# Eight of twelve `w_ada` column blocks summed on GpSimd instead of multiplied on TensorE, in a transformer block on one Trainium2 core

## What is computed

```python
cond = jax.nn.silu(c)                                  # [1, 1024]
mod = cond @ w_ada[l] + b_ada[l]                       # w_ada: [1024, 6 * 1024]
sh_m, sc_m, g_m, sh_f, sc_f, g_f = jnp.split(mod[:, None, :], 6, axis=-1)
h = _rms(x, norm_mix[l]) * (1.0 + sc_m) + sh_m
proj = h @ w_in[l]                                     # attention, index, SSM, gates
...                                                    # top-k attention and a Mamba2 scan
mixed = jax.nn.sigmoid(g_attn) * y_attn + jax.nn.sigmoid(g_ssd) * y_ssd
x = x + g_m * (mixed @ w_out[l])
h = _rms(x, norm_ffn[l]) * (1.0 + sc_f) + sh_f
x = x + g_f * _moe(h, ...)                             # 32 experts, top 4, 384 MiB of weights
```

## Time and profile before

| | |
|---|---|
| median of the runs | 2021.14 us |
| the profiled execution | 2021.23 us, its span 2019.4 us (1.8 us lie around the span) |
| PE busy | 1940.4 us of the span (96%) |
| DVE busy | 658.3 us |
| ACT busy | 406.2 us |
| POOL busy | 64.9 us |
| DMA | 582.19 MB, mean 288 GB/s |

### The profile page before, as it was taken

One profiled execution on the slowest core, in us unless ns is written; L12 is line 12 of the kernel. 1 busy time (PEld: TensorE's weight loads), 2 busy tenths in 40 slices (PEclk: granted clock), 3 DMA queues, 4 the chain that ended last, 5 costly groups with the idle time before them and its releaser, 6 DMA issues.

```text
span 2019.4 us, 22293 instructions
## 1 busy us (share of the span) xinstructions
PE 1940.4 (96%) x8948; PEld 1104.6 (55%) x8948; DVE 658.3 (33%) x1358; ACT 406.2 (20%) x861; POOL 64.9 (3%) x93
## 2 busy tenths in 40 slices
PE   7999999999999999988999999999999999999998
PEld 3767885333333333333333333766888456778863
DVE  1487513122122122121211222552333435433353
ACT  2134213111110111111101112253211033422110
POOL 0000000000000000000000000210011011001100
PEclk9999999999999999999999999999999999999999
DMA  9855358999999999999999999263443434335440
GB/s 352 293 203 194 133 211 348 414 433 430 434 430 434 432 432 432 430 434 431 432 434 430 431 428 413 75 229 104 165 154 138 171 111 172 120 125 167 142 171 22
DMA packets 119863, 582.19 MB, mean 288 GB/s; under 512 B 5544, under 2 KB 51760, under 8 KB 106352
## 3 DMA queue, kind: packets, MB, share of 16 engines
q1 hardware_dynamic: 118128, 574.65, 70.9%
q0 software_dynamic: 1664, 6.56, 1.0%
HBM read 580.13 MB, written 2.63 MB: 289 GB/s over the span
## 4 chain that ended last, share of the span: by engine, by line
PE 75%; DMA 20%; DVE 3%; ACT 1%; issue 0%; SPq 0%; DVEq 0%; ACTq 0%
PE psum L362 51%; PE psum L707 11%; PE psum L640 9%; DMA ring<-w_gu 9%; DMA work<-w_gu 9%; DMA ring<-w_dn 2%; PE psum L2260 1%; DVE work L1901 1%; PE psum L694 1%; PE psum L678 1%; PE psum L1118 0%; DMA ring<-w_ada 0%; PE psum L1160 0%; PE psum L1149 0%; DVE work L1899 0%
## 5 line engine op out<-in xcount | busy, mean ns | idle before, releaser
L362 PE MATMUL psum<-normed,ring 128*128 128x256 f32 (+1 forms) x2400 | 498.8, 369 | 0.1
L362 PEld LDWEIGHTS psum<-normed,ring 128*128 128x128 f32 x2400 | 435.6, 191 | 59.2 <-issue 4.4
L640 PE MATMUL psum<-work,normed 128*64 128x512 f32 x1024 | 233.2, 609 | 26.6 <-DMA work<-w_gu 26.6
L640 PE MATMUL psum<-ring,normed 128*64 128x512 f32 x1024 | 233.0, 609 | 24.0 <-DMA ring<-w_gu 22.8
L362 PE MATMUL psum<-work 128*128 128x128 f32 (+7 forms) x1216 | 222.5, 353 | 0.2 <-ACT work L1482 0.2
L362 PE MATMUL psum<-ring,work 128*128 128x512 f32 (+1 forms) x464 | 197.5, 578 | 0.1
L362 PEld LDWEIGHTS psum<-work 128*128 128x128 f32 (+2 forms) x1216 | 147.7, 185 | 84.5 <-issue 73.5
L640 PEld LDWEIGHTS psum<-work,normed 128*64 128x64 f32 x1024 | 78.0, 140 | 179.6 <-issue 177.6
L640 PEld LDWEIGHTS psum<-ring,normed 128*64 128x64 f32 x1024 | 75.0, 140 | 179.1 <-issue 161.1
L362 PE MATMUL psum<-ring,normed 128*128 128x512 f32 (+1 forms) x368 | 152.1, 567 | 0.7 <-PE psum L362 0.4
L362 PEld LDWEIGHTS psum<-ring,work 128*128 128x128 f32 x464 | 87.4, 190 | 100.0 <-issue 98.7
(11 more groups left out here) (339 smaller groups left out, 1372.1 us busy)
## 6 DMA issues: line engine op xcount, KB each, us to landing
work<-w_gu SPq DMA_DIRECT2D x31, 4096.0 KB, 29.8
ring<-w_gu SPq DMA_DIRECT2D x29, 4096.0 KB, 30.0
work<-w_dn SPq DMA_DIRECT2D x15, 4096.0 KB, 29.8
ring<-w_dn SPq DMA_DIRECT2D x14, 4096.0 KB, 30.1
ring<-w_in SPq DMA_DIRECT2D x23, 2048.0 KB, 9.9
ring<-w_up SPq DMA_DIRECT2D x44, 1024.0 KB, 7.3
ring<-w_down SPq DMA_DIRECT2D x10, 2048.0 KB, 7.8
ring<-w_ada SPq DMA_DIRECT2D x8, 2048.0 KB, 9.1
```

The costliest lines, as they stand in the source:

```text
L362: return pe.matmul(out, lhsT, rhs, start=first, stop=last, **kw)
L640: ins = pe.matmul(b[r], self.hgT[:, 2 * q + k, r], w[:, 2 * k + e, n0:n0 + 512], start=q == 0 and k == 0, stop=q == QUARTERS - 1 and k == ...
```

## The change

Only the eight late blocks and what serves them change.

- PE no longer computes `ada(4)` to `ada(11)`, ACT no longer copies them (`ada_part`). POOL does: for each of the eight row chunks of a block it multiplies `128x512` by a column of `cond` (a `tensor_scalar`, in place in the ring but for the first) and adds it to the sum (a `tensor_tensor`), each waiting for the one before (`step`): 8 multiplications and 7 additions per block. The order of the blocks is `ADA_ORDER` = 6, 7, 4, 5, 8, 9, 10, 11. A block comes in two halves of 1 MiB, fetched by POOL's own DMAs into slot 3 (`ADA_SLOT`); a half of the next block is issued when that half of the present one has been used.
- The first two (6, 7) stand ahead of the bias-table DMAs in POOL's program, the other six behind the wait for `w_ready` 2 and the four constant loads.
- `mod_rows` and `sum_mod` stay on PE, wait for `acc_ready` n, raised after the n-th block, and those of 4, 5, 8, 9, 10, 11 stand later: ahead of `attn_out`, ahead of its third pair, between the `ys`, and in the router. DVE's `take_rows`, `take_mod` and `scale_columns` follow them. The copies of 10 and 11 stand late on ACT.
- The other front weights take slots 0 to 2 by a table. The second half of the experts' first quarter goes into slot 3, behind a wait for `acc_ready` 8 and behind the second and third quarter in SP's queue; its first half waits for `ys` 3 and not for `ys` 1.
- On the host, all front weights are laid out so that each partition's part of a slot is contiguous (16 KB a row and no more 2 or 4 KB), `w_in`'s first blocks and `ada_first`'s included; each is one DMA.

```diff
@@ front_banks, front_slots
-    u += [("ga", 6), ("a", 10), ("ga", 7), ("ya", 0), ("ya", 1)] + [("yT", 0, j) for j in range(2)] + [("m", 10)]
-    u += [("ya", 2), ("a", 11)] + [("yT", 1, j) for j in range(2)] + [("ya", 3), ("m", 11)]
-    u += [("ys", p) for p in range(4)]
+    u += [("ga", 6), ("ga", 7), ("m", 4), ("ya", 0), ("ya", 1)] + [("yT", 0, j) for j in range(2)] + [("m", 5)]
+    u += [("ya", 2)] + [("yT", 1, j) for j in range(2)] + [("ya", 3)]
+    u += [("ys", 0), ("m", 8), ("ys", 1), ("ys", 2), ("m", 9), ("ys", 3)]
+            ("win", 2): 1, ("win", 3): 2, ("wkv",): 0, ("win", 4): 1, ("win", 5): 2,
+            ("win", 6): 0, ("gate", 0): 1, ("win", 7): 2, ("gate", 1): 0, ("gate", 2): 1, ("gate", 3): 2,
+            ("wo",): 0, ("wso", 0): 1, ("wso", 1): 2, ("wout", 0): 0, ("wout", 1): 1}
+ADA_SLOT = 3
+ADA_ORDER = (6, 7, 4, 5, 8, 9, 10, 11)
@@ sync
-        X.load_when_free(sp, io, SP, PAIR_SLOTS[0], [slot_used(("wso", j)) for j in range(2)])
+        X.load_first(sp, io, SP, slot_used(("wso", 1)), 0)
         sp.wait_ge(mixed_ready, 4)
-        for j in range(2):
-            sp.wait_ge(*B.released("m", 10 + j))
+        sp.wait_ge(*B.ready("m", 9))
         for name in PAIR_SLOTS[1:3]:
             X.load(sp, io, SP, name, 0)
+        X.load_first(sp, io, SP, (acc_ready, len(ADA_ORDER)), 1)
         X.load_when_free(sp, io, SP, PAIR_SLOTS[3], [slot_used(("wout", j)) for j in range(2)])
@@ gpsimd
+        def load_half(n, half):
+            src = io["w_ada"][ADA_ORDER[n] - 4][:, 2048 * half:2048 * half + 2048]
+            pool.dma_start(ada_w[:, half].rearrange("p k n -> p (k n)"), src).then_inc(ada_half[half], 16)
+
+        def sum_columns(n):
+            out = ada_sum(ADA_ORDER[n])
+            if n >= 6:
+                pool.wait_ge(*B.ready("yx", 1))
+            elif n >= 3:
+                pool.wait_ge(*B.ready("m", ADA_ORDER[n - 3]))
+            elif n == 0:
+                pool.wait_ge(*B.ready("mod", 1))
+                pool.wait_ge(cond_ready, 1)
+            for half in range(2):
+                pool.wait_ge(ada_half[half], 16 * (n + 1))
+                for i in range(4):
+                    k = 4 * half + i
+                    w = ada_w[:, half, i]
+                    step(pool.tensor_scalar(w if k else out, w, cond[:, k, 0:1], None, ALU.mult))
+                    if k:
+                        step(pool.tensor_tensor(out, out, w, ALU.add))
+                if n + 1 < len(ADA_ORDER):
+                    load_half(n + 1, half)
+            pool.nop().then_inc(acc_ready, 1)
         pool.wait_ge(*S.ready("bottom"))
         bias_rows(2)
+        pool.wait_ge(ada_done, 2)
+        for half in range(2):
+            load_half(0, half)
+        for n in range(2):
+            sum_columns(n)
...
+        for n in range(2, len(ADA_ORDER)):
+            sum_columns(n)
         pool.wait_ge(x1_used, 1)
@@ tensor
-        def ada(j):
-            w = wait_slot("ada", j)
-            pe.wait_ge(*B.empty("a", j))
-            for k in range(KC):
-                g = k % 4
-                ins = matmul(pe, bank("a", j)[32 * g:32 * g + 32], cond[:, k], w[:, k], k < 4, k >= 4)
-            ins.then_inc(*B.fills("a", j))
         def mod_rows(j):
-            pe.wait_ge(ada_in, j - 1)
+            pe.wait_ge(acc_ready, ADA_ORDER.index(j) + 1)
             pe.wait_ge(*B.empty("m", j))
-            matmul(pe, bank("m", j), ones, acc[:, j % 3]).then_inc(*B.fills("m", j))
+            matmul(pe, bank("m", j), ones, ada_sum(j)).then_inc(*B.fills("m", j))
@@ vector, two of the places
-                take_rows(5, 1)                      # was inside the softmax of query tile 0
...
+        take_rows(4, 0)
+        gate_attention(0)
+        gate_attention(1)
+        take_rows(5, 1)
```

More of the change, by code:

```diff
@@ L66 @@
 D_IN = C_GATE + 2 * D
+WIN_COLS = [C_XBC + 512 * j for j in range(3)] + [C_Z + 512 * j for j in range(2)] + [C_GATE + 512 * j for j in range(4)]
 class Layout:
@@ L134, with __init__ @@
 class Uses:
-    def __init__(self, full, free, names, inc=1, base=None, twice=(), first=0):
+    def __init__(self, full, free, names, inc=1, base=None, twice=(), first=0, places=None):
         n = len(full)
@@ L305, in by_pair, with block, blocks, first_ada @@
     return v.reshape(PAIRS, parts, P, k * 2 * n)
+def block(w, c0, n):
+    return np.asarray(w)[:, c0:c0 + n].reshape(-1, P, n).transpose(1, 0, 2).reshape(P, -1)
+def blocks(w, starts, n=512):
+    return np.stack([block(w, c0, n) for c0 in starts])
+def first_ada(w):
+    return w[:, 0:2 * D].reshape(2, 4, P, 2, 2, 512).transpose(4, 0, 2, 1, 3, 5).reshape(4, P, 4096)
+def first_in(w):
+    return np.stack([blocks(w[r:r + 512], (0, 512)) for r in (0, 512)])
 def lay_out(i):
@@ L820, in first_block @@
     B = Uses(bank_full, bank_free, front_banks())
-    S = Uses(slot_full, slot_full, front_slots(), inc=16, twice={("win", 2): 2, **{("ada", j): 4 for j in range(4)}})
-    BP = Uses(bank_full, bank_free, PAIR_BANKS, base=B.after(), first=1)
+    S = Uses(slot_full, slot_full, front_slots(), inc=16, places=front_slots())
+    BP = Uses(bank_full, bank_free, PAIR_BANKS, base=B.after(), first=FIRST_PAIR_BANK)
     SP = Uses(place_full, place_full, PAIR_SLOTS, inc=16, first=1)
@@ L940, in slot_used, with wait_free @@
                              "wout": ("x1", 1, 2 * j) if kind == "wout" else None}[kind])
-        def load(src, *name):
-            if order.index(name) >= SLOTS:
-                sp.wait_ge(*slot_used(order[order.index(name) - SLOTS]))
-            k, n = src.shape[0] // P, src.shape[1]
-            sp.dma_start(slot(S.no(name), k, n), kpm(src)).then_inc(*S.fills(*name))
-        win = [(C_Q, 512), (C_KV, 512), (C_QI + 256, 328)] + [(C_XBC + 512 * j, 512) for j in range(3)] + \
-              [(C_Z + 512 * j, 512) for j in range(2)]
+        def wait_free(name):
+            earlier = held.get(S.no(name))
+            if earlier is not None:
+                sp.wait_ge(*slot_used(earlier))
+            held[S.no(name)] = name
@@ L1369, in tensor @@
         gate(0)
-        ada(10)
         gate(1)
+        mod_rows(4)
         pe.wait_ge(*S.ready("wo"))
@@ L1375, in tensor @@
         y_transposes(0)
-        mod_rows(10)
+        mod_rows(5)
         attn_out((2,))
-        ada(11)
         y_transposes(1)
         attn_out((3,))
-        mod_rows(11)
         pe.wait_ge(*B.released("yT", 1, 1))
-        for j in range(2):
-            w = wait_slot("wso", j)
-            by_feature(("ys", 2 * j), w, 0, yT)
-            by_feature(("ys", 2 * j + 1), w, 256, yT)
+        w = wait_slot("wso", 0)
+        by_feature(("ys", 0), w, 0, yT)
+        sum_mod(8)
+        by_feature(("ys", 1), w, 256, yT)
+        w = wait_slot("wso", 1)
+        by_feature(("ys", 2), w, 0, yT)
+        sum_mod(9)
+        by_feature(("ys", 3), w, 256, yT)
         w = [wait_slot("wout", j) for j in range(2)]
@@ L1686, in scalar @@
         token_rows(1)
+        for half in range(2):
+            take(late_rows[:, half], bank("m", 10 + half), "m", 10 + half)
         act.wait_ge(route_ready, 1)
```

182 lines of the change are left out of this document (83 added, 99 removed).

## The result

The changed kernel takes 2074.06 us (median of 6 runs, 2073.82 to 2075.35) against 2021.02 for the kernel before in runs on the same chip (6 runs, 2020.5 to 2022.12): a ratio of 1.0262, 95% interval 1.0252 to 1.0272. It is slower, as forecast, but by 53 us and not by 5, and it lies outside the range of 2013 to 2041. The profiled execution has a span of 2072.1 us.

A forecast was written before the change was run, and what follows sets the result against it. Experts were taken as bound by their weight stream, following PE's start on them. POOL's pace, four blocks of 16.6 plus 3.5 of delays minus 65.1, shifts that by +4.8: 2021.2 + 4.8 = 2026.0 us, range 2013 to 2041.

The forecast's parts named there:

- The bound of the kernel before: Experts bound by their weight stream at 431 GB/s; the front by PE, then DVE, then PE up to the routing.
- the places of PE's savings: PE work removed before, beside and behind DVE's part; without waits PE starts on experts 11.0 us earlier.
- above, the two-input addition, 1.34: Upper bound for one `tensor_scalar` on POOL, whose time was taken as 0.75 us in each block.
- X: Extra delay of POOL or PE from engine interference, slow PE after idle and hand-overs; taken as 3.5 us.
- 4P + X: PE's start on experts shifts by four POOL block times (16.6 each) plus X, minus 65.1: +4.8 us.
- Rival 3: Much slower: `tensor_scalar` costs what `tensor_tensor` does and DVE and POOL block each other; +28, either alone +15 to +20; chance 0.18.
- Rival 4: DMA: half blocks landing in 9.8 us or later beside expert weights make the last two blocks late; no chance of its own.
- A later than S - 9: Eighth block's end, put at 331, decides through slot 3 only if later than 340, with PE's experts starting near 349.
- S + 899: The experts' stage ends 899 us after PE starts on experts, so a shift of that start moves the end equally.
- if the stage of the experts does not follow S: Sign that the forecast is wrong: the experts' end does not move along with PE's start on experts.
- The rule weighed there, one input "roughly line-rate": Skill page's rule for POOL: one-input operation about 0.6 us with the wait, block 15.4, kernel level with before.
- The exclusion rule: Two-SBUF-input DVE instructions and POOL instructions reading SBUF exclude each other; would make X near 8, time near 2030.5.

The follow-up runs named there:

- The kernel with five blocks: Changed kernel with blocks 4, 5, 6 back on PE, five on POOL, and bias loads on SP's queue: 2012.51 us, ratio 0.9962 to the kernel before.
- the last kernel with five blocks: Five blocks on POOL, but slot 3's expert half asked for at once and biases back at the end of POOL's list: 2007.61 us, ratio 0.9932.

## Why the prediction was wrong, point by point

- **The bound of the kernel before, and the places of PE's savings**: right. With POOL fast enough (seven products left out) PE's first expert product comes 10.9 earlier (331.82 for 342.74) and the issue of w_dn 10.5, against 11.0 predicted. The kernel with five blocks can be compared only behind `w_ready` 2: from there to the projection it takes 63.3 us where it was 69.9, 6.6 less, and the prediction's terms without its two `sum_mod` give 8.5 - 2.0 = 6.5. `w_ready` 2 came at 223.56 for 224.4, the third block started at 226.77 for 227.6. The first weights gained 0.4, within 0 to 0.8.
- **The step that failed**: "above, the two-input addition, 1.34". An instruction that no row showed was bounded above by one with more inputs, in the belief that the second input is what costs. It costs 1.65. With eight products the block is 8 x (1.65 - 0.75) = 7.2 longer than 16.6; DMA issues and gaps are the other 0.6 to 24.4. Four blocks lie between the third block's start and the projection: 4 x 7.8 = 31.2. The case against it, a memset with no input at 0.31 for 256 columns, was a lower bound; nothing in the trace was an upper one, and the range should have said so.
- **X**: 3.5 taken, 5.9 measured. Of it 2.1 is POOL's four blocks beyond 4 x 24.4: in the third block, beside DVE's chain of chunk 1, two products take 2.14 and 2.61, and it lasts 26.7. Another 0.3 is the hand-over, and 3.5 is PE at the granted clock of 0.50 (the 32 passes at 328.53 take 2.9 more, `sum_mod(9)` 1.87 for 1.10). Together 31.2 + 2.4 - 0.8 (the earlier `w_ready` 2) = 32.8, and 305.5 + 32.8 = 338.3, the measured start of the projection. The structure, the pace 4P + X, held at P = 24.4 and 20.0, and at 13.5 PE waited for almost nothing.
- **Rival 3** (the product costs what the addition does, and the engines block each other) was the right direction, with 0.18, and still 25 us short at its ends (1.65 against 1.34; a shift of 28). Its "either of them +15 to +20" does not follow from the prediction's own formula, which gives +24 for P 21.3 with X 3.5 and +9 for P 16.6 with X 8.
- **Rival 4**, "I give it no chance of its own", and the rule that the eighth block decides only by its slot (A later than S - 9): wrong twice. By that rule A = 381.4 would cost 0.9 us at S = 389.5. But the end of the last block is also a wait of PE, `mod_rows(11)` ahead of the experts (7.11), and what stands behind it in POOL's list, the biases, has a deadline too (5.0). At A = 331 both were far off; at 381 most of the 10.0 ahead of the experts' first product and of the 6.2 behind it is theirs. Only the 5 of the biases could be taken away by itself; the rest goes with POOL's lateness.
- **S + 899**: the sign "if the stage of the experts does not follow S" came true. S, PE's start on experts (344.36), is 389.50 in the changed kernel, 45.1 later, and the end is 53.0 later. What did hold is the step behind it, that the stream is full from the issue of w_dn (359.09) on. The last load of the stage, from the chain of the kernel before and of the changed one:

```profile
1215.94 31.42 DMA ring<-w_dn
```

```profile
1270.00 30.26 DMA ring<-w_dn
```

  They land at 1247.36 and 1300.26, in both 888.3 us behind the issue of w_dn (359.09 and 412.00). The same distance is 888.2 in the last kernel with five blocks, 888.3 with the products as `tensor_tensor`, 888.2 with three blocks earlier. It is 890.5, 891.8 and 892.6 in the three kernels in which SP issues the biases ahead of expert weights. So with five blocks w_dn was issued 12.3 earlier and only 8.4 reached the end, and 12.8 and 13.5 once the biases were back in POOL's list.
- **Where the miss lies**: of 52.9 - 4.8 = 48.1 us, 32.8 had come about by the start of the projection (31.2 the product's price) and 15.3 behind it (10.0 + 6.2 for the 0.9 of the prediction), in the late half block, the late biases and PE's clock behind these waits.
- The rule weighed there, one input "roughly line-rate" (Trainium skill, GPSIMD Engine Reference, "4.1 Engine selection"), fits the copy (0.61) and not the `tensor_scalar` (1.56, 2.5 times as much). The exclusion rule holds here, but it cost 2.1 us where X had up to 8; it costs more where DVE sets the pace, as the three runs with POOL beside it show.

What stays open: why `tensor_scalar` is so dear on POOL was not found; only that neither the operand nor the operation matters. How the 10.0 and 6.2 divide was not shown beyond the 5 us of the biases.

## What to carry to other kernels

An operation that the trace doesn't show has no upper bound from one that looks more expensive: when work goes to another engine, measure its exact form there first, in an idle stretch of the old kernel. Compare the new engine's pace with the distance between its deadlines, not its sum with the whole, and move only as many pieces as it can deliver (five of eight here); put them where the engine that it disturbs is not the bound. When an engine becomes late, look at what stands behind the work in its queue, at the transfers that now run into each other, and at the memory that frees late.

## What the runs showed of the hardware

- On POOL at 128x512 in float32: `tensor_scalar` 1.56 us, `tensor_tensor` 1.27, `tensor_tensor` with a broadcast column 1.04, copy 0.61, memset about 0.53.
- POOL beside DVE costs DVE 0.3 to 0.4 us for each 128x256 instruction that meets an addition of 128x256; beside POOL's 128x512 products with a broadcast column (1.04 us) even a 128x64 `tensor_scalar` of DVE takes 0.98 to 1.31. Memsets slow only the instructions with one input. 46 us of additions on memory that nobody uses cost the kernel 13 us, 28 products or 90 memsets some 5.
- A DMA of 1 MiB issued by POOL lands in 7.5 us with little else on its way, and in 17.9 behind 10 MiB that SP had issued 10 to 13 us earlier; it landed when the queues had all but run empty (the DMA share falls from 1.17 at 361 to 366 us to 0.01 behind 370). With 8 MiB of these held back it landed in 7.5.
- Behind a wait of 7.56 us PE's granted clock is 0.50 (1.2 GHz) from 326.8 to 331.0 though it is busy throughout, and 0.98 from 334.0 to 338.2. The two passes right behind a wait of 10.91 take 2.08 for 1.02, the 32 passes at 328.53 9.91 for 7.0.
